# Column sums of the opening taken off TensorE, x's chunk 1 loaded early, and three orders of work changed, in a one-layer S5, dilated-attention and memory block

## The reference

```python
h = rms_norm(x, norm_g)                       # x * rsqrt(mean(x*x, -1) + eps) * g
proj = h @ w_in                               # 1024 -> 8704: 68 tiles of 128 columns
u_ssm, z_ssm, q, k, v, z_attn, q_mem, z_mem, gate_logits = split(proj)
y = gelu(s5_ssm(u_ssm, ...)); y = y * sigmoid(y @ w_glu + b_glu); o_ssm = y * silu(z_ssm)
o_attn = dilated window attention, 12 heads in 3 groups, softmax-weighed, * silu(z_attn)
kv_mem = rms_norm(mem, mem_norm_g) @ w_mem_kv # 256 memory tokens, k and v of 4 heads
o_mem = softmax(q_mem @ k_mem.T) @ v_mem * silu(z_mem)
gates = sigmoid(gate_logits + b_gate)
x = x + (gates0*(o_ssm@w_br_ssm) + gates1*(o_attn@w_br_attn) + gates2*(o_mem@w_br_mem)) @ w_out
return rms_norm(x, final_norm_g)
```

## Time and profile before

| | |
|---|---|
| median of 3 runs | 2515.33 us (2513.67 to 2515.53) |
| profiled execution | 2515.46 us, span of the trace 2513.7 us |
| TensorE busy | 2484.8 us, 99% of the span |
| VectorE, ScalarE, GpSimd busy | 56%, 23%, 8% |
| granted TensorE clock | 0.997 of full, mean |

### The profile page before, as it was taken

How to read it: one execution, slowest core, us unless ns; L and a number is a source line. 1 busy time by engine, 2 the same in 40 slices (tenths; PEclk the granted TensorE clock), 3 DMA queues, 4 the chain that set the end, 5 groups by cost and what they waited for, 6 DMA issues and landing times.

```text
span 2513.7 us, 31563 instructions
## 1 busy us (share of the span) xinstructions
PE 2484.8 (99%) x12520; PEld 2008.8 (80%) x12520; DVE 1406.8 (56%) x2586; ACT 589.3 (23%) x1266; POOL 192.8 (8%) x332
## 2 busy tenths in 40 slices
...
GB/s 195 92 79 82 116 91 126 124 98 107 107 141 134 140 161 156 164 146 59 126 89 114 114 146 131 133 212 243 211 216 180 245 182 172 246 176 236 164 227 64
DMA packets 171990, 373.40 MB, mean 149 GB/s; under 512 B 26943, under 2 KB 72099, under 8 KB 165956
## 3 DMA queue, kind: packets, MB, share of 16 engines
...
...
## 4 chain that ended last, share of the span: by engine, by line
PE 94%; DMA 3%; DVE 2%; ACT 0%; issue 0%; POOL 0%; SPq 0%; DVEq 0%; ACTq 0%
PE bank L136 28%; PE bank L138 27%; PE bank L137 27%; PE bank L2090 2%; PE bank L2054 1%; DMA w_raw<-w_br 1%; PE bank L1903 1%; PE bank L2111 1%; PE bank L2133 1%; PE bank L2069 1%; PE bank L2008 1%; PE bank L2011 1%; PE bank L1994 1%; DMA xa<-x_t 1%; PE bank L2121 1%; PE bank L1972 0%
## 5 line engine op out<-in xcount | busy, mean ns | idle before, releaser
L136 PE MATMUL bank<-h_hi,w_hi 128*128 128x512 f32 (+1 forms) x2720 | 1084.1, 399 | 7.4 <-DVE w_lo L130 5.7
L138 PE MATMUL bank<-h_hi,w_lo 128*128 128x512 f32 (+1 forms) x2720 | 1058.1, 389 | 0.0
L137 PE MATMUL bank<-h_lo,w_hi 128*128 128x512 f32 (+1 forms) x2720 | 1056.9, 389 | 0.0
L136 PEld LDWEIGHTS bank<-h_hi,w_hi 128*128 128x128 f32 x2720 | 511.3, 188 | 129.5 <-issue 21.2
L138 PEld LDWEIGHTS bank<-h_hi,w_lo 128*128 128x128 f32 x2720 | 510.9, 188 | 108.4
L137 PEld LDWEIGHTS bank<-h_lo,w_hi 128*128 128x128 f32 x2720 | 511.6, 188 | 103.2 <-issue 1.7
L128 DVE CAST w_hi<-w_raw 128x1024 fp32r<-128x1024 f32 (+1 forms) x122 | 83.9, 688 | 322.7 <-PE bank L138 299.6
L136 PE MATMUL bank<-h_hi 128*128 128x512 f32 (+1 forms) x464 | 172.3, 371 | 1.1 <-DVE xq L1833 1.1
L138 PE MATMUL bank<-h_hi,h_lo 128*128 128x512 f32 (+1 forms) x464 | 170.4, 367 | 0.0
L137 PE MATMUL bank<-h_lo,h_hi 128*128 128x512 f32 (+1 forms) x464 | 170.4, 367 | 0.0
L885 POOL DMA_DIRECT2D proj_d<-ev x160 | 88.6, 554 | 947.3 <-ACT ev L1063 575.8
...
## 6 DMA issues: line engine op xcount, KB each, us to landing
...
```

The source lines that it names most:

```text
L136: nc.tensor.matmul(out, ah, bh, start=(start and n == 0), stop=False)
L137: nc.tensor.matmul(out, ah, bl, start=False, stop=False)
L138: last = nc.tensor.matmul(out, al, bh, start=False, stop=(stop and n == len(pairs) - 1))
```

## The change

The diff has five parts. (1) The 8 squares of a job are added elementwise into the first, by VectorE for job 0 and by GpSimd for the others (`add_squares`). `sum_squares` then makes one column of sums for each 128 tokens, root and reciprocal work on 2 or 4 columns, VectorE multiplies them into a diagonal (`diag`), and one matmul with `ones` spreads them over the partitions (`spread`). The scalings read that PSUM bank. (2) The memory tokens get a room of their own, and x's chunk 1 is loaded at the start. (3) All four engines that compute get another order of work in the opening. (4) In attention, `scores` goes ahead of `output`. (5) At the start of the merge, the pieces for k-tiles 0 to 4 are split after the last GLU unit and after the second weight slot, and k-tile 5 comes third in its group.

```diff
-KV_BANK = (1, 5, 6, 7)
+KV_BANK = (6, 7, 6, 7)
+SUM_BANK = (2, 3, 2, 3, 3)
...
-          (slice(2, 4), h_room[:, :, :], 1), (slice(4, 5), stage[:, 2:3, :], 3)])
-N_FIRST = len(FIRST) + 1
+          (slice(5, 6), zs(KS - 1)[:, 0:CW].unsqueeze(1), None), (slice(2, 4), h_room[:, :, :], 1),
+          (slice(4, 5), stage[:, 2:3, :], 3)])
+N_FIRST = len(FIRST)
...
-first = [8, 9, 10, 11, 6, 7] if q == 0 else [9, 10, 11, 6, 7, 8]
-return first if b == 1 else list(range(k0, k1))
+if b == 1:
+    return [8, 9, 10, 11, 6, 7] if q == 0 else [9, 10, 11, 6, 7, 8]
+if b == 2 and q == 0:
+    return [0, 1, 5, 2, 3, 4]
+return list(range(k0, k1))
...
-xbuf = (xa, xb)
+mb = mem_room[:, :].rearrange("p (k c) -> p k c", k=KD)
+xbuf = (xa, mb, xb, xa, xb)
...
+F0 = 2 * len(jobs)
+def add_squares(queue, engine, j):
+    w = jobs[j][0]
+    for k in range(1, KD):
+        queue.wait_ge(sq_ready, 8 * j + k + 1)
+        if k > 1:
+            queue.wait_ge(sq_used, 7 * j + k - 1)
+        engine.tensor_tensor(sq[:, 0, 0:w], sq[:, 0, 0:w], sq[:, k, 0:w], ALU.add).then_inc(sq_used, 1)
...
+load_x(2, slice(0, KD), yr_loaded[3])
...
+for j in range(1, len(jobs)):
+    add_squares(pool, nc.gpsimd, j)
...
-act.wait_ge(x_loaded[j % 2], 16 * (j // 2 + 1))
+act.wait_ge(*((x_loaded[0], 16), (x_loaded[1], 16), (yr_loaded[3], 16), (x_loaded[0], 32),
+              (x_loaded[1], 32))[j])
...
-        act.wait_ge(sq_used, 8 * (j - 1) + k + 1)
-    nc.scalar.activation(sq[:, k, 0:w], xbuf[j % 2][:, k, 0:w],
+        act.wait_ge(sq_used, 7 * (j - 1) + max(k, 1))
+    nc.scalar.activation(sq[:, k, 0:w], xbuf[j][:, k, 0:w],
...
-w = jobs[j][0]
-act.wait_ge(sq_used, 8 * (j + 1))
+n = jobs[j][0] // P
+act.wait_ge(f_mm, 2 * j + 1)
...
-nc.scalar.activation(rstd[:, j % 2, 0:w], psum[2 + j % 2][:, 0:w], ACT.Sqrt,
+nc.scalar.activation(rcol[:, j % 2, 0:n], psum[SUM_BANK[j]][:, 0:n], ACT.Sqrt,
...
-    act.wait_ge(kv_mm, 2 * j)
-nc.scalar.activation(h_of(h_hi, j)[:, ks, :], xbuf[j % 2][:, ks, 0:w],
+    act.wait_ge(kv_mm, (0, 0, 0, 4, 8)[j])
+nc.scalar.activation(h_of(h_hi, j)[:, ks, :], xbuf[j][:, ks, 0:w],
...
-act.wait_ge(h_ready, 2 * (j - 1))
-act.dma_start(xbuf[j % 2][:, :, :], x_t[:, :, jobs[j][2]]).then_inc(x_loaded[j % 2], 16)
+act.wait_ge(h_ready, (0, 0, 0, 2, 6)[j])
+act.dma_start(xbuf[j][:, :, :], x_t[:, :, jobs[j][2]]).then_inc(x_loaded[(j + 1) % 2], 16)
...
-act.wait_ge(yr_loaded[c], 16 if c < 3 else 48)
+act.wait_ge(yr_loaded[c], 16 if c < 3 else 16 + 48)
...
 squares(0)
 root(0)
 squares(1)
+hi_parts(0)
 root(1)
-hi_parts(0)
-load_x(2)
-hi_parts(1)
 load_x(3)
 squares(2)
 root(2)
+hi_parts(1)
+squares(3)
 keep_kv(0)
+hi_parts(2)
+load_x(4)
 keep_kv(1)
-squares(3)
-hi_parts(2)
 root(3)
-load_x(4)
 keep_kv(2)
-keep_kv(3)
 squares(4)
 hi_parts(3)
 root(4)
+keep_kv(3)
 hi_parts(4)
 act.wait_ge(h_ready, 2 * len(jobs))
 for c in range(NQ):
...
-if i == len(FIRST):
+ks, src, slot = FIRST[i]
+if slot is None:
...
-    src, ks = zs(KS - 1)[:, 0:CW].unsqueeze(1), slice(5, 6)
...
-    ks, src, slot = FIRST[i]
...
-        if u == NQ * KS - 2:
-            for i in range(5, 8):
-                first_hi(i)
-first_hi(8)
+for i in range(5, N_FIRST):
+    first_hi(i)
...
     w, gi = jobs[j][0], jobs[j][4]
+    n = w // P
     dve.wait_ge(root_done, j + 1)
-    r = rstd[:, j % 2, 0:w]
+    r = rcol[:, j % 2, 0:n]
     nc.vector.reciprocal(r, r).then_inc(rstd_done, 1)
-    dve.wait_ge(rstd_done, j + 1)
-    x = xbuf[j % 2]
+    dve.wait_ge(rstd_done, 2 * j + 1)
+    nc.vector.tensor_tensor(diag[:, j % 2, 0:n, :], ident[:, :].unsqueeze(1).to_broadcast((P, n, P)),
+                            r.unsqueeze(2).to_broadcast((P, n, P)), ALU.mult).then_inc(rstd_done, 1)
+def scaled_parts(j):
+    w, gi = jobs[j][0], jobs[j][4]
+    dve.wait_ge(f_mm, 2 * j + 2)
+    r = psum[SUM_BANK[j]][:, 0:w]
+    x = xbuf[j]
     for k in range(KD):
...
 def low_parts(j):
-    w, x = jobs[j][0], xbuf[j % 2]
+    w, x = jobs[j][0], xbuf[j]
     for half in range(2):
...
                                 ALU.subtract).then_inc(h_ready, 1)
 def split_kv(n):
-    used = (lambda s: (kv_mm, 2 * (n - 1))) if n >= 2 else None
+    used = (lambda s: (kv_mm, 6)) if n == 3 else None
     split_pair(dve, n + 1, used, into=(kv_half(h_hi, n), kv_half(h_lo, n)))
+add_squares(dve, nc.vector, 0)
 split_pair(dve, 0, None, slots=(0,))
 normalised(0)
+scaled_parts(0)
+normalised(1)
 split_pair(dve, 0, None, slots=(1,))
-normalised(1)
+scaled_parts(1)
 split_kv(0)
+normalised(2)
+scaled_parts(2)
 split_kv(1)
 split_kv(2)
-normalised(2)
+normalised(3)
+scaled_parts(3)
 split_kv(3)
-normalised(3)
 normalised(4)
+scaled_parts(4)
 steps_done = [0]
 def link(ins):
...
 if u == NQ * KS - 1:
-    for i in range(5, 8):
-        first_lo(i)
     split_pair(dve, N_MRG, lambda s: (g_mm, NQ * KS), slots=(1,), loads=N_MRG + 1)
...
-first_lo(8)
+for i in range(5, N_FIRST):
+    first_lo(i)
...
+    n = jobs[j][0] // P
+    if j >= 2:
+        pe.wait_ge(scaled, (0, 0, 8, 16, 32)[j])
+    pe.wait_ge(sq_used, 7 * (j + 1))
+    for t in range(n):
+        mm = nc.tensor.matmul(psum[SUM_BANK[j]][:, t:t + 1], sq[:, 0, P * t:P * (t + 1)],
+                              ones[:, 0:1], start=True, stop=True)
+    mm.then_inc(f_mm, 1)
+def spread(j):
+    pe.wait_ge(rstd_done, 2 * j + 2)
...
-    if j >= 2:
-        pe.wait_ge(root_done, j - 1)
-    for k in range(KD):
-        pe.wait_ge(sq_ready, 8 * j + k + 1)
-        nc.tensor.matmul(psum[2 + j % 2][:, 0:w], ones[:, :], sq[:, k, 0:w],
-                         start=(k == 0), stop=(k == KD - 1)).then_inc(sq_used, 1)
+    nc.tensor.matmul(psum[SUM_BANK[j]][:, 0:w], ones[:, :],
+                     diag[:, j % 2, 0:w // P, :].rearrange("p n c -> p (n c)"),
+                     start=True, stop=True).then_inc(f_mm, 1)
...
+    if n >= 2:
+        pe.wait_ge(kv_out, 2 * (n - 1))
...
-if s == 0 and c == 1:
-    pe.wait_ge(kv_out, 2)
-if s == 0 and c >= 2:
-    pe.wait_ge(root_done, len(jobs) + 2 - c)
-if s == 1 and c >= 1:
+if s == 0 and c == 2:
+    pe.wait_ge(scaled, 24)
+if s == 1 and c >= 2:
...
     turn(t)
+t = step_at(beat, 0)
+if t is not None:
+    scores(t)
 t = step_at(beat, 5)
...
     output(t)
-t = step_at(beat, 0)
-if t is not None:
-    scores(t)
 if beat == A_END:
...
 warm(16)
 sum_squares(0)
+warm(4)
+spread(0)
+warm(8)
 sum_squares(1)
-warm(28)
+warm(8)
 first_tiles(0, 0)
+spread(1)
+sum_squares(2)
 first_tiles(1, 0)
-sum_squares(2)
-for n in range(3):
-    memory_kv(n)
+spread(2)
+memory_kv(0)
+first_tiles(0, 1)
 sum_squares(3)
-first_tiles(0, 1)
+first_tiles(1, 1)
+memory_kv(1)
+spread(3)
+memory_kv(2)
+first_tiles(0, 2)
+sum_squares(4)
 memory_kv(3)
-first_tiles(1, 1)
-sum_squares(4)
-for c in (2, 3):
-    for s in range(2):
-        first_tiles(s, c)
+first_tiles(1, 2)
+spread(4)
+for s in range(2):
+    first_tiles(s, 3)
 for n in range(2, NT):
     for c in range(NQ):
```

More of the change, by code:

```diff
@@ L102, in build_program @@
         w_raw = sb(ctx, "w_raw", [P, 2, KD, P])
-        k_mem = sb(ctx, "k_mem", [P, MH, ML])
-        v_mem = sb(ctx, "v_mem", [P, 2, MH * MD])
+        mem_room = sb(ctx, "mem_room", [P, KD * ML])
+        k_mem = mem_room[:, 0:MH * ML].rearrange("p (h m) -> p h m", h=MH)
+        v_mem = mem_room[:, MH * ML:].rearrange("p (s m) -> p s m", s=2)
         w_loaded = [sem(f"w_loaded{s}") for s in range(2)]
@@ L309, in build_program @@
                 sq = sb(pn, "sq", [P, KD, CW])
-                rstd = sb(pn, "rstd", [P, 2, CW])
+                diag = sb(pn, "diag", [P, 2, CW // P, P])
+                rcol = sb(pn, "rcol", [P, 2, CW // P])
             with ExitStack() as pn:
@@ L453, in piece_of_first @@
         def piece_of_first(k):
-            return 8 if k == 5 else [i for i, f in enumerate(FIRST) if f[0].start <= k < f[0].stop][0]
+            return [i for i, f in enumerate(FIRST) if f[0].start <= k < f[0].stop][0]
         def piece_of_later(k):
@@ L501, in kv_half @@
         def kv_half(t, n):
-            flat = t[:, 2 + n % 2, :, :].rearrange("p k c -> p (k c)")
-            return flat[:, KD * ML:].rearrange("p (s k m) -> p s k m", s=2, k=KD)
+            flat = t[:, (2, 2, 3, 3)[n], :, :].rearrange("p k c -> p (k c)")
+            half = flat[:, 0:KD * ML] if n == 1 else flat[:, KD * ML:]
+            return half.rearrange("p (s k m) -> p s k m", s=2, k=KD)
         def h_of(t, j):
@@ L522, in load_x @@
                     w, src, cols = jobs[j][0:3]
-                    sp.dma_start(xbuf[j % 2][:, ks, 0:w], src[:, ks, cols]).then_inc(loaded, 16)
+                    sp.dma_start(xbuf[j][:, ks, 0:w], src[:, ks, cols]).then_inc(loaded, 16)
                 load_x(0, slice(0, KD // 2), x_loaded[0])
```

17 lines of the change are left out of this document (9 added, 8 removed).

## The result

The changed kernel takes **2538.45 us** (median of 4 runs, 2537.5 to 2539.01) against 2514.91 for the kernel before on the same chip: ratio 1.0088, 95% interval 1.0076 to 1.0101. The prediction said 2526, 2518 to 2535: slower, as forecast, but by 23.5 us and not by 11, and outside the range.

A forecast was written before the change was run, and what follows sets the result against it. The prediction took TensorE, busy for 99% of the span, as the bound, then its waits. From 2515.4 us, opening +20.6, attention -3.5 and merge -6.9 gave 2525.6, about 2526 us; range 2518 to 2535 for 8 in 10.

The forecast's parts named there:

- clock term: Opening: TensorE's granted clock drops behind long idle stretches, adding 6.5 us, between 0 and 10.
- The stalls and what ends them: Opening: TensorE waits some 50 us against some 10 before, ending it 14.1 us later without clock drops.
- Rival (a): Opening: the clock does not fall in idle stretches; opening +14.1, total 2519 us; chance 0.12.
- hand-over count: Opening: each start is the later of engine's last end and awaited end, durations from profile rows; opening ends at 136.4 us.
- Rival (c): Opening: VectorE and GpSimd hinder each other, 1.2 and 0.8 us at two places; total 2528 us; chance 0.15.
- GpSimd's add: Opening: one 512-wide two-input add on GpSimd takes 1.18 us, bounds 0.69 and 2.25.
- Rival (b): Opening: GpSimd is slow, near 2.25 us an add; total 2536 us; chance 0.15.
- One-column passes: Opening sums: a TensorE pass of one column takes 0.11 us, between 0.03 and 0.43.
- Parts 2 and 3: Attention saves 3.5 us by one operand-shape change fewer in 38 beats; the merge saves 6.9 us, its wait and clock drop.
- Rival (d): Opening: saved TensorE work decides; 23 us shorter, total 2482 us if waits do not grow; chance 0.08 with smaller waits.

The follow-up runs named there:

- filled kernel: The changed kernel with thrown-away products of ones filling nearly all of TensorE's idle time in the opening: 2532.28 us, ratio 1.0061.
- run of ScalarE's order: The changed kernel with ScalarE's order alone rewritten, high parts ahead of memory-product copies and next squares, root 3 ahead of a copy: 2515.46 us, ratio 0.9993.
- run with short adds: The changed kernel with GpSimd's adds cut to the first 128 columns of each job, so output is not the reference's: 2525.88 us, ratio 1.0036.
- direct sums: The changed kernel with column sums of chunks 0 and 1 made by TensorE from the eight squares, without VectorE's and GpSimd's adds there: 2539.55 us, ratio 1.0084.
- kernel of the orders: The changed kernel with ScalarE's, TensorE's and VectorE's written orders in the opening changed, same instructions: 2508.12 us, ratio 0.9968.
- best2: The kernel of the orders with constants awaited later, second weight split earlier, diagonals 1 and 3 between split halves, spread(4) directly behind its sums: 2497.50 us, ratio 0.9923.

## Why the prediction was wrong in size

Start of TensorE's steps in us. The filled kernel has the changed kernel's orders at nearly the full clock (one low stretch, from 23.4 to 26.8 us), as the prediction's count without its clock term:

| step | predicted | changed kernel | filled (fill_more) |
|---|---|---|---|
| `first_tiles(0, 0)` | 30.2 | 32.75 | 33.50 |
| `sum_squares(2)` | 42.5 | 46.94 | 47.74 |
| `spread(2)` | 52.0 | 61.96 | 61.95 |
| `first_tiles(0, 1)` | 63.7 | 75.75 | 73.80 |
| `spread(3)` | 83.3 | 97.38 | 93.50 |
| `first_tiles(0, 2)` | 99.3 | 113.86 | 110.00 |
| `spread(4)` | 116.8 | 134.17 | 130.34 |
| `first_tiles(0, 3)` | 125.5 | 142.94 | 139.10 |
| opening ends | 136.4 | 156.37 | 150.06 |

- **The stalls and what ends them** were right, each in its place. Those behind the queues' orders were right in size too: 5.1, 9.4 and 7.9 us forecast ahead of chunks 1 to 3, 4.96, 9.60 and 7.74 found; the first two are what the run of ScalarE's order cut to 2.0. Those behind adds and splits were too short: 6.4 forecast ahead of `sum_squares(2)` and 3.2 ahead of `spread(2)`, 8.05 and 5.79 found.
- **The clock term**, 6.5 us, was right in kind and in sum: 6.2 by the medians, 6.3 by the filled kernel's opening, 7.8 with its later start taken off. By places it was partly luck: 1.9 at and behind `spread(2)`, in the memory product, were not in the forecast (clock 0.50 from 60 to 66 us), 2.5 instead of 1.6 came at chunk 3, and the 1.6 at chunk 2 came to nothing, since the split of the last pair set the end there. Rival (a), no fall, is refuted: clock 0.80 in the first 122 us.
- **The step that failed is the durations in the hand-over count**: they were taken from rows in which no other engine was in the way. The last column is 13.7 us behind the first at the end. It loses 3.3 by the first tiles (constants 1.9 later than counted, of which 1.5 is this execution's later start and no fault of the count; VectorE's adds 0.78 and not 0.71 apart, 0.5; the first spread in 2.08 us at the low clock, 1.0), 1.9 by `sum_squares(2)` (adds of 1.43 and not 1.18), **4.7** by `spread(2)` (the split and the diagonal beside the adds), 0.7 up to `first_tiles(0, 2)` and 2.8 by `spread(4)` (2.0 of it the wait for the split of the last pair, which ran beside the adds of chunk 3).
- **Rival (c)** named the mechanism, with 2.0 us and a chance of 0.15, and looked for it at two places only: the low half of chunk 2 behind an add in progress, and the first add of job 2 behind a split. Its cost is about 6 us (the run with short adds). It had to be in the forecast, at every cast and every VectorE row with two SBUF inputs that overlaps an add. With that the sum would have been near 2532 (an estimate, 2526 and these 6), inside the range's upper half; the rest of the miss is the longer adds and the later chain to the first tiles. The Trainium skill's rule in "Who interferes with whom" pointed at these instructions, and the prediction used it for a rival only.
- **GpSimd's add**, 1.18: 1.43 from one to the next with VectorE quiet. The estimate by the Trainium skill, GPSIMD Engine Reference, section 3.1, 1.1 to 1.2 us, is too low for this case by about a fifth; the measurement decides. Rival (b), 2.25, is wrong too.
- **One-column passes**, 0.11, were right: 0.10 at the full clock (eight from 83.24 to 84.05 us), 0.107 in the direct sums, 0.2 at the low clock.
- **Parts 2 and 3** (attention and merge): -10.4 forecast, -11.3 found behind the opening. The merge's wait and drop are gone, as counted; attention gives some 5 by the trace and not 3.5, since `scores`, too, take 1.02 instead of 1.06 us up to the next product, now that this is `output`'s and not the tile's.
- **Rival (d)**: the saved work did not decide here. In the kernel of the orders TensorE is busy for 93.7 us of the first 125, and its opening still ends at 125.2, 2.9 us behind the old one; it is faster than before by parts 4 and 5 alone. Only in best2, at 114.5, is the opening shorter.

Sum: 14.1 forecast without the clock, 13.7 by the last column and 6.3 for the clock make 34.1 for the opening, and -11.3 behind it: +22.8, as the spans say. With the late start of 1.5 us counted to the clock the shares are 12.2 and 7.8.

What stays open: only one of the clashes was taken away by itself, the first split's; how the 23 us of ScalarE's order divide between its places, since all were moved at once; and whether the old sums in the best order would do as well as the new.
